# Two transformer blocks on one core: spreading the convolution's taps, two divisions and the weight splits over the attention loop by another table

## The chip, the cores and the metric

The kernel runs on one core of one Trainium2 chip. The metric is the device time of one execution in microseconds (us). Of the kernel before there are three timed runs, 1228.01, 1232.46 and 1233.43 us, with the median 1232.46 us. One further execution was profiled and took 1230.22 us. The engines are called TensorE (PE in the profile, PEld for its weight loads), VectorE (DVE), ScalarE (ACT), GpSimd (POOL) and SyncE (SP, which here only issues DMAs). The five engines run their own instruction queues in order and meet at semaphores only.

## The reference, cut to what matters

The program computes a first block (a gated pool and a chunked recurrence), and a second block on its output. The change lies in the second block's mixer, where an attention of 8 heads over 768 keys and a depthwise convolution of 31 taps over 512 channels are independent of one another until they meet in one projection:

```python
def dwconv(x, w, b):                       # k = 31 taps, 512 channels
    y = lax.conv_general_dilated(x, w[:, None, :], window_strides=(1,), padding=[(k // 2, k // 2)],
                                 dimension_numbers=('NWC', 'WIO', 'NWC'), feature_group_count=x.shape[-1])
    return y + b

def attend(q_nope, q_rope, k_nope, k_rope, v):
    s = (jnp.einsum('bqhd,bkhd->bhqk', q_nope, k_nope)
         + jnp.einsum('bqhr,bkr->bhqk', q_rope, k_rope)).astype(jnp.float32) * SOFTMAX_SCALE
    p = jax.nn.softmax(s, axis=-1).astype(v.dtype)
    return jnp.einsum('bhqk,bkhd->bqhd', p, v)

    attn_l = attend_blocked(q_nope_l, q_rope_l, ...)
    conv_l = conformer_conv(u_l, ...)      # silu(layer_norm(dwconv(a * sigmoid(g))))
    y_l = merge_groups(conv_l, attn_l, w_o[i], b_o[i])
```

## The kernel before, in words

Every engine has its own program, written out as a Python function that issues the engine's instructions in their final order; there is no scheduler. The attention is a loop over heads `h` 0 to 7 and six key tiles `t` 0 to 5 of 128 keys, and this pair (h, t), a step, is the unit in which work is placed on every engine.

TensorE computes in each step the scores of one key tile (three fp32r matmuls for the split operands, and a fourth that subtracts the row maximum through the diagonal tile DGR) and then multiplies the previous tile's exponentials (PR, which lie in PTA) with the values. In steps 1 to 4 it also computes two matmuls for the maxima of the next head (128 queries by 768 keys, tile PB). In step 2 it projects the queries of head h+2 (9 matmuls), in step 5 of an even head the keys of the next pair of heads (12 matmuls), and in steps (1, 3), (1, 4) and (2, 3) tiles of the values (12 short matmuls each). TensorE's program is not changed.

VectorE reduces the maxima (`maxima`, TENSOR_REDUCE of PB into PX), rotates the queries (`query`, TMPQ), computes the low halves of queries, keys and weights (HL, KL, WL; `split` is the weights' one and follows ScalarE's copy of the high half, WH), divides the finished pairs of heads (`pair`), and fills what is left with taps of the convolution (SCALAR_TENSOR_TENSOR on CV, one instruction per tap and group of 128 channels, 124 in all, 88 of them in this loop). How many taps follow each step is a table, `conv_step`; `conv_plan` deals the taps out in that order, alternating between two channel groups as long as there are two. Four places matter. The maxima of head h+1 for query tile j use one pair of PSUM banks for all j, so TensorE's maxima matmuls j+1 wait until VectorE has reduced j. The first score matmul group of head h+1 ends with DGR, which ScalarE makes from VectorE's fourth reduction of head h. The query projection in an odd head writes the bank from which VectorE reads `key_low(h + 2)`, and so waits for it. And `conv("end")` leaves nothing over: the last tap is at (7, 2).

ScalarE computes the exponential of each step (`power_of`, PTA), DGR (`maxima`), the high halves (KH, HH, WH), the copies of finished heads (`values_out`), and for each pair of heads the reciprocal of the denominators as Exp(-Ln(x)) (`divisors`), for which it loads one activation table and then the other back. `conv_square` squares a finished channel group two steps after its last tap (`CONV_END`), and GpSimd then adds the sums of groups 1 and 2 on VP and DG.

SyncE fetches the weight blocks; it waits for VectorE's splits (semaphore v_w), three buffers ahead.

Of the kernel before, what the change touches and what calls it, by code (L numbers as in the profile page):

```python
# [355 lines left out]
def build_in(nc, ctx, A, out, consts, masks):  # L356
# [152 lines left out]
    def raw_of(n):  # L509
        return RAW[n % NRAW]  # L510
# [44 lines left out]
    GLU_AT = {1: "82", 2: "84", 3: "86"}  # L555

    def conv_step(h, t):
        return 5 if h == 7 else (3, 2, 1, 1, 1, 3)[t] if h % 2 == 0 else (2, 1, 2, 1, 2, 3)[t]

    def conv_plan():  # L560

# [199 lines left out]
    def act_prog(e):  # L761
        a = Eng(e)

        def split(nb):

            if nb >= len(BLOCKS):
                return
            n, at, size = BLOCKS[nb]
            a.wait_ge(S_.raw[n % NRAW], n)
            if nb >= NW:  # L770
                a.wait_ge(S_.p_blk, nb - NW)
            a.copy(WH[nb % NW][:, 0:size], raw_of(n)[:, at:at + size]).then_inc(S_.a_w, nb)
# [367 lines left out]
        def key_high(h):  # L1140

            for part, (lo, hi) in enumerate(((NCTX, NKEY), (0, NCTX))):
                a.wait_ge(S_.p_blk, KEY_BLOCK[h // 2])
                if h > 2:
                    a.wait_ge(S_.p_sm, ("s", h - 3, 5))
                z = main.of(("k", h // 2, part))
                op = a.copy(KH[h % 3][0:64, lo:hi], z[64 * (h % 2):64 * (h % 2) + 64, 0:hi - lo])
            op.then_inc(S_.a_h, ("k", h))

        def query_high(h):  # L1150
            a.wait_ge(S_.v_ev, ("q", h))
            if h > 2:
                a.wait_ge(S_.p_sm, ("s", h - 3, 5))
            a.copy(QH[h % 3], TMPQ[:, :]).then_inc(S_.a_h, ("q", h))

        def value_tiles(g, q):
            if q < 2:
                a.wait_ge(S_.p_sm, ("v", g, q))
            else:
                a.wait_ge(S_.p_blk, VALUE_BLOCK[g])  # L1160
            a.wait_ge(S_.v_h, ("cq", 2))
            a.wait_ge(S_.v_h, ("kr", 2))
            z = main.of(("v", g, q))
            for i in range(2):
                op = a.copy(VGs[:, 2 * q + i, 2 * g:2 * g + 2, 0:3:2, :],
                            z[:, 256 * i:256 * i + 256].rearrange("p (a s n) -> p a s n", a=2, s=2))
            op.then_inc(S_.a_ev, ("v", g, q))

        def maxima(h, j):

            c = 4 * (h % 2) + j
            a.wait_ge(S_.v_ax, ("mx", h, j))
            if h > 1:
                a.wait_ge(S_.p_sm, ("s", h - 2, 5))
            a.act(DGR[h % 2][:, js(j)], IDN[:, :], ACTF.Identity, scale=NM[:, c:c + 1]).then_inc(S_.a_s, ("dgr", h, j))

        def power_of(h, t):
            s = 6 * h + t
            a.wait_ge(S_.p_sm, ("s", h, t))
            if s > 2:  # L1180
                a.wait_ge(S_.p_sm, ("o", (s - 3) // 6, (s - 3) % 6))
            a.act(PR[s % 3], main.of(("s", h, t)), ACTF.Exp, scale=SCALE).then_inc(S_.a_ev, ("s", h, t))

        def values_out(h):

            me, other = ((0, 64), (64, 128)) if h % 2 == 0 else ((64, 128), (0, 64))
            z = aux.of(("ov", h))
            a.wait_ge(S_.p_sm, ("o", h, 5))
            i = h // 2 % 2
            if h > 3:  # L1190
                a.wait_ge(S_.v_h, ("m", 4 + h // 2 - 2))
            a.copy(OTS[i][me[0]:me[1], :], z[me[0]:me[1], :])
            a.copy(SU[i][me[0]:me[1], :], z[other[0]:other[1], :]).then_inc(S_.a_ax, ("ov", h))

        def divisors(*pairs):

            for p in pairs:
                a.wait_ge(S_.a_ax, ("ov", 2 * p + 1))
                a.act(SU[p % 2], SU[p % 2], ACTF.Ln).then_inc(S_.a_s, ("sul", p))
            for p in pairs:  # L1200
                a.wait_ge(S_.a_s, ("sul", p))
                a.act(SU[p % 2], SU[p % 2], ACTF.Exp, scale=-1.0).then_inc(S_.a_s, ("su", p))

        def pair_high(p):
            a.wait_ge(S_.v_s, ("pair", p))
            a.copy(MH[:, 4 + p, :], OTS[p % 2]).then_inc(S_.a_h, ("m", 4 + p))

        def conv_square(j):
            a.wait_ge(S_.v_cv, ("cv", j))
            if j == 0:  # L1210
                a.wait_ge(S_.p_sm, "rqd")
            if j > 1:
                a.wait_ge(S_.g_cv, ("n2", min(j, 3) - 1))
            a.act(DG[:, :] if j else VP[:, 0, 0:512], CV[:, j, :], ACTF.Square).then_inc(S_.a_cv, ("sq", j))
# [18 lines left out]
        for h in range(8):  # L1233
            for t in range(6):
                power_of(h, t)
                if t == 0 and h % 2 and h < 6:
                    key_high(h + 2)
                    split(KEY_BLOCK[(h + 1) // 2] + NW)
                if t == 1 and h:
                    values_out(h - 1)  # L1240
                if 1 <= t <= 4 and h < 7:
                    maxima(h + 1, t - 1)
                if t == 4 and h in (3, 5):
                    pair_high((h - 3) // 2)
                if t == 3 and h < 6:
                    split(QUERY_BLOCK[h + 2] + NW)
                if t == 4 and h < 6:
                    query_high(h + 2)
                if (h, t) in ((1, 4), (1, 5), (2, 4)):
                    value_tiles(1, (h + t) - 5 if h == 1 else 2)  # L1250
                if (h, t) == (2, 4):
                    split(VALUE_BLOCK[1] + NW)
                if t == 5 and h in (2, 4):
                    divisors(h // 2 - 1)
                if t == 5 and h % 2 == 0 and h < 6:
                    key_high(h + 2)
                for j in range(4):
                    if CONV_END[j] != "end" and 6 * CONV_END[j][0] + CONV_END[j][1] + 2 == 6 * h + t < 44:
                        conv_square(j)
# [79 lines left out]
    def dve_prog(e):  # L1339
        v = Eng(e)  # L1340

        def split(nb):

            if nb >= len(BLOCKS):
                return
            n, at, size = BLOCKS[nb]
            v.wait_ge(S_.a_w, nb)
            i = nb % NW
            v.tt(WL[i][:, 0:size], raw_of(n)[:, at:at + size], WH[i][:, 0:size].bitcast(F32), SUB).then_inc(S_.v_w, nb)
# [450 lines left out]
        def query(h):  # L1800

            v.wait_ge(S_.p_blk, QUERY_BLOCK[h])
            if h:
                v.wait_ge(S_.v_h, ("q", h - 1))
            v.tt(TMPQ[:, :], main.of(("q", h)), CS[:, NCTX:NKEY], MUL).then_inc(S_.v_ev, ("q", h))
# [4 lines left out]
        def key_low(h):  # L1810
            v.wait_ge(S_.a_h, ("k", h))
            for part, (lo_, hi) in enumerate(((NCTX, NKEY), (0, NCTX))):
                z = main.of(("k", h // 2, part))[64 * (h % 2):64 * (h % 2) + 64, 0:hi - lo_]
                v.tt(KL[h % 3][0:64, lo_:hi], z, KH[h % 3][0:64, lo_:hi].bitcast(F32), SUB)\
                    .then_inc(S_.v_ev, *[("k", h // 2, part)] * (h % 2), *[("kl", h)] * part)

        def maxima(h, j):
            c = 4 * (h % 2) + j
            v.wait_ge(S_.p_sm, ("mx", h, j))
            if h > 1:  # L1820
                v.wait_ge(S_.a_s, ("dgr", h - 2, j))
            v.maxneg(NM[:, c:c + 1], PB[2 + (j % 2 if h == 0 else 0)][:, 0:NKEY]).then_inc(S_.v_ax, ("mx", h, j), ("mx2", h, j))

        def pair(p):

            v.wait_ge(S_.a_s, ("su", p))
            v.tt(OTS[p % 2], OTS[p % 2], SU[p % 2], MUL).then_inc(S_.v_s, ("pair", p))
# [18 lines left out]
        for h in range(8):  # L1846
            for t in range(6):
                if 1 <= t <= 4 and h < 7:
                    maxima(h + 1, t - 1)
                if t == 0 and h % 2 and h < 6:  # L1850
                    key_low(h + 1)
                    split(KEY_BLOCK[(h + 1) // 2] + NW)
                if t == 1 and h % 2 and h < 6:
                    key_low(h + 2)
                if t == 3 and h in (3, 5):
                    pair((h - 3) // 2)
                if t == 3 and h < 6:
                    query(h + 2)
                    split(QUERY_BLOCK[h + 2] + NW)
                if t == 5 and h < 6:  # L1860
                    query_low(h + 2)
                if t == 5 and h in (3, 5):
                    pair_low((h - 3) // 2)
                if t == 5 and h == 2:
                    split(VALUE_BLOCK[1] + NW)
                conv((h, t))
# [697 lines left out]
```

## Time and profile before

| | before |
|---|---|
| median of three runs | 1232.46 us |
| the profiled execution | 1230.22 us, span 1228.4 us |
| TensorE busy, weight loads busy | 1139.7 us (93%), 928.2 us (76%) |
| VectorE busy | 864.3 us (70%) |
| ScalarE busy | 550.5 us (45%) |
| GpSimd busy | 164.4 us (13%) |
| attention loop | about 660 to 797 us of the span |

Busy times are shares of one span and say nothing of a single stage. The attention loop takes 137 us, about 11% of the span; in the timeline of the trace a step can be told by its value matmul, the row PB<-PTA,VG, which starts after the scores of the step that follows.

### The profile page before, as it was taken

To read this page: it belongs to the slowest core of one execution; us is meant where nothing else is said; L and a number is where in the kernel's file an instruction comes from. 1 tells how busy PE (TensorE), PEld (TensorE's weight loads), DVE (VectorE), ACT (ScalarE), POOL (GpSimd) and SP (SyncE) were. 2 spreads that over 40 slices of the span, in tenths; PEclk is the share of its full clock that TensorE was granted. 3 is DMA by queue.
4 is the path that set the end of the run, shared out by engine and by line. 5 is a ranking of instruction groups with operands and counts; after the bars stand their busy time and mean duration, and the time that the engine had idled before them with its cause. 6 is when DMAs were issued, how large, how long until landed. Compare 5 with 4: busy or idle time off the path is not lost.

```text
span 1228.4 us, 14076 instructions
## 1 busy us (share of the span) xinstructions
PE 1139.7 (93%) x5488; PEld 928.2 (76%) x5488; DVE 864.3 (70%) x1352; ACT 550.5 (45%) x851; POOL 164.4 (13%) x179
## 2 busy tenths in 40 slices
PE   1869999999999989989999988998999999999996
PEld 1658888888888868879887755577888888888885
DVE  5868899988877774464888887967666656655236
ACT  3265455445433342776425565454643444432221
POOL 0034433344423210010010000000000000000001
PEclk9999999999999999999999999999999999999999
DMA  7723233233244566563211010112232222234211
GB/s 291 303 107 138 75 132 137 73 134 137 103 146 163 190 244 144 194 36 109 73 45 46 3 66 35 35 34 103 91 116 87 86 102 103 104 103 164 94 35 68
DMA packets 28306, 136.59 MB, mean 111 GB/s; under 512 B 7760, under 2 KB 8016, under 8 KB 14416
## 3 DMA queue, kind: packets, MB, share of 16 engines
q1 hardware_dynamic: 20448, 128.46, 29.8%
q10 hardware_dynamic: 7792, 7.24, 2.6%
q8 instruction: 43, 0.70, 0.2%
q14 instruction: 23, 0.19, 0.0%
HBM read 133.57 MB, written 2.12 MB: 110 GB/s over the span
## 4 chain that ended last, share of the span: by engine, by line
PE 66%; DVE 16%; ACT 10%; DMA 3%; issue 3%; POOL 1%; ACTq 0%; DVEq 0%; SPq 0%
PE PB L185 66%; DVE RAW L1365 3%; ACT WH L199 2%; ACT L200 2%; DMA RAW<-in_wstream 2%; DVE WL L206 2%; DVE CV L214 1%; DVE XL L214 1%; DVE SS L214 1%; DVE PX L237 1%; DMA XL<-in_xT 1%; DVE HB L231 1%; POOL UPA L206 1%; PE PB L193 1%; ACT HH L199 1%
## 5 line engine op out<-in xcount | busy, mean ns | idle before, releaser
L185 PE MATMUL PB<-HH,WH 128*128 128x512 f32 (+1 forms) x896 | 354.3, 395 | 18.8 <-DVE WL L206 8.3
L206 DVE TENSOR_TENSOR WL<-RAW,WH 128x1024 fp32r<-128x1024 f32 (+2 forms) x174 | 202.6, 1172 | 203.9 <-ACT WH L199 203.2
L185 PE MATMUL PB<-HH,WL 128*128 128x512 f32 (+1 forms) x896 | 343.6, 384 | 0.0
L185 PE MATMUL PB<-HL,WH 128*128 128x512 f32 (+1 forms) x896 | 343.4, 383 | 0.0
L199 ACT ACTIVATE WH<-RAW 128x1024 fp32r<-128x1024 f32 (+2 forms) x174 | 169.5, 981 | 297.5 <-PE PB L185 263.0
L185 PEld LDWEIGHTS PB<-HH,WH 128*128 128x128 f32 x896 | 171.6, 192 | 54.4 <-DVE WL L206 9.0
L185 PEld LDWEIGHTS PB<-HH,WL 128*128 128x128 f32 x896 | 171.2, 191 | 33.4
L185 PEld LDWEIGHTS PB<-HL,WH 128*128 128x128 f32 x896 | 171.8, 192 | 29.3 <-issue 0.5
L214 DVE SCALAR_TENSOR_TENSOR CV<-VP,PC,CV 128x512 f32<-128x512 f32 x120 | 89.1, 778 | 0.7
L206 POOL TENSOR_TENSOR PX<-PX,NPOW 128x2 f32<-128x2 f32 (+2 forms) x7 | 6.2, 893 | 474.7 <-DVE PX L206 428.4
L185 PE MATMUL PB<-WH,AH 128*128 128x512 f32 x176 | 68.5, 389 | 0.0
L185 PE MATMUL PB<-WL,AH 128*128 128x512 f32 x176 | 68.5, 389 | 0.0
L185 PE MATMUL PB<-WH,AL 128*128 128x512 f32 x176 | 68.5, 389 | 0.0
L206 POOL TENSOR_TENSOR PTA<-HB 128x256 f32<-128x256 f32 (+1 forms) x53 | 46.3, 898 | 124.4 <-DVE HB L231 112.3
L1365 DVE CUSTOM_DVE_ANT_0 RAW<-RAW,CR,PC 128x1024 f32<-128x1024 f32 x48 | 62.1, 1309 | 0.0
L185 PE MATMUL PB<-PTA,VG 128*128 128x512 f32 x96 | 51.5, 621 | 7.0 <-ACT PTA L200 7.0
L200 ACT ACT_TABLE_LOAD x43 | 55.2, 1283 | 6.1 <-DMA PC<-in_params 5.4
L185 PE MATMUL PB<-WH,HH 128*128 128x512 f32 x128 | 51.9, 406 | 2.2 <-DVE WL L206 1.4
L206 POOL TENSOR_TENSOR UPA<-HB 128x256 f32<-128x256 f32 (+1 forms) x51 | 45.0, 907 | 50.8 <-DVE HB L231 41.3
L200 ACT ACTIVATE PTA<-PTA 128x512 f32<-128x512 f32 x51 | 32.0, 627 | 42.4 <-POOL PTA L206 40.7
L185 PE MATMUL PB<-WL,HH 128*128 128x512 f32 x128 | 50.4, 394 | 0.0
L185 PE MATMUL PB<-WH,HL 128*128 128x512 f32 x128 | 50.3, 393 | 0.0
(270 smaller groups left out, 1855.1 us busy)
## 6 DMA issues: line engine op xcount, KB each, us to landing
RAW<-in_wstream SPq DMA_DIRECT2D x108, 1024.0 KB, 4.8
RAW<-in_wstream SPq DMA_DIRECT2D x5, 768.0 KB, 4.2
RAW<-in_wstream SPq DMA_DIRECT2D x5, 512.0 KB, 3.5
XL<-in_xT SPq DMA_DIRECT2D x2, 1024.0 KB, 8.1
HB<-in_x SPq DMA_DIRECT2D x2, 1024.0 KB, 6.3
out<-XL SPq DMA_DIRECT2D x8, 256.0 KB, 2.0
ROWS<-in_rows ACTq DMA_DIRECT2D x3, 512.0 KB, 7.9
XC<-in_ctx SPq DMA_DIRECT2D x1, 1024.0 KB, 7.0
```

Source lines behind the costliest of these rows:

```text
L185: return self.put(lambda e: e.matmul(o, l, r, start=start, stop=stop, skip_group_check=skip))
L193: return self.put(lambda e: e.transpose(o, i, idn))
L199: return self.put(lambda e: e.activation(o, i, f))
L200: return self.put(lambda e: e.activation(o, i, f, bias=bias, scale=scale))
L206: return self.put(lambda e: e.tensor_tensor(o, a, b, op))
L214: return self.put(lambda e: e.scalar_tensor_tensor(out=o, in0=a, scalar=s, in1=b, op0=o1, op1=o2))
L231: return self.put(lambda e: e.tensor_tensor_scan(o, a, b, 0.0, MUL, ADD))
L237: return self.put(lambda e: e.tensor_reduce(o, i, AX.X, ALU.max, negate=True))
L1365: v.put(lambda e: e.tensor_tensor_reduce(out=PROD if vec == "cc" else w, in0=w, in1=ROW[vec], scale=1.0, scalar=col(bias, j + i), op0=MUL, ...
```

## The change

In one table and two loops the change moves work; it adds and removes no instruction of the computation.

```diff
     def conv_step(h, t):
-        return 5 if h == 7 else (3, 2, 1, 1, 1, 3)[t] if h % 2 == 0 else (2, 1, 2, 1, 2, 3)[t]
+        return 5 if h == 7 else (2, 2, 5 if h < 6 else 2, 0, 1, 4)[t] if h % 2 == 0 else (1, 1, 5, 0, 1, 2)[t]
```

ScalarE's loop:

```diff
                 power_of(h, t)
+                if t == 2 and h in (2, 4):
+                    divisors(h // 2 - 1)
...
-                if t == 4 and h in (3, 5):
-                    pair_high((h - 3) // 2)
+                if t == 5 and h in (2, 4):
+                    pair_high(h // 2 - 1)
...
-                if t == 5 and h in (2, 4):
-                    divisors(h // 2 - 1)
```

VectorE's loop:

```diff
-                if t == 3 and h in (3, 5):
-                    pair((h - 3) // 2)
+                if t == 4 and h in (2, 4):
+                    pair(h // 2 - 1)
                 if t == 3 and h < 6:
                     query(h + 2)
+                if t == 4 and h < 6:
                     split(QUERY_BLOCK[h + 2] + NW)
                 if t == 5 and h < 6:
                     query_low(h + 2)
-                if t == 5 and h in (3, 5):
+                if t == 0 and h in (3, 5):
                     pair_low((h - 3) // 2)
```

The first place is VectorE's queue in head 3, from the second reduction for head 4 (step 2) to the first reduction for head 5 (in head 4, step 1). Before:

```order
L237 TENSOR_REDUCE PX<-PB 128x1
L214 SCALAR_TENSOR_TENSOR CV<-VP,PC,CV 128x512 x2
L237 TENSOR_REDUCE PX<-PB 128x1
L206 TENSOR_TENSOR OT<-OT,TMP 128x512
L206 TENSOR_TENSOR TMPQ<-PB,CS 128x512
L206 TENSOR_TENSOR WL<-RAW,WH 128x1024
L214 SCALAR_TENSOR_TENSOR CV<-VP,PC,CV 128x512
L237 TENSOR_REDUCE PX<-PB 128x1
```

In the changed kernel, the same stretch:

```order
L237 TENSOR_REDUCE PX<-PB 128x1
L211 TENSOR_SCALAR CV<-VP,PC 128x512
L214 SCALAR_TENSOR_TENSOR CV<-VP,PC,CV 128x512 x4
L237 TENSOR_REDUCE PX<-PB 128x1
L206 TENSOR_TENSOR TMPQ<-PB,CS 128x512
L237 TENSOR_REDUCE PX<-PB 128x1
L206 TENSOR_TENSOR WL<-RAW,WH 128x1024
L214 SCALAR_TENSOR_TENSOR CV<-VP,PC,CV 128x512
L206 TENSOR_TENSOR HL<-TMPQ,HH 128x512
L214 SCALAR_TENSOR_TENSOR CV<-VP,PC,CV 128x512 x4
L237 TENSOR_REDUCE PX<-PB 128x1
```

Five taps instead of two stand between the second and the third reduction; the fourth reduction has passed the division (OT), the split of a weight block (WL) and a tap; and four taps instead of six stand ahead of the first reduction for the next head (before, that stretch reads HL<-TMPQ, HL<-OT, six taps, TENSOR_REDUCE).

The second place is ScalarE's queue around the divisions of the first pair. Before, at the end of head 2 and the begin of head 3 (PTA<-PB is a step's exponential, TMP holds the denominators):

```order
L200 ACTIVATE PTA<-PB 128x512
L200 ACT_TABLE_LOAD
L200 ACTIVATE TMP<-TMP 128x512
L200 ACT_TABLE_LOAD
L200 ACTIVATE TMP<-TMP 128x512
L199 ACTIVATE KH<-PB 64x512
L199 ACTIVATE KH<-PB 64x256
L200 ACTIVATE PTA<-PB 128x512
```

In the changed kernel, at steps (2, 2) and (2, 3):

```order
L200 ACTIVATE PTA<-PB 128x512
L200 ACT_TABLE_LOAD
L200 ACTIVATE TMP<-TMP 128x512
L200 ACT_TABLE_LOAD
L200 ACTIVATE TMP<-TMP 128x512
L200 ACTIVATE DGR<-IDN,PX 128x128
L200 ACTIVATE PTA<-PB 128x512
L200 ACTIVATE DGR<-IDN,PX 128x128
```

The two table loads and two activations no longer stand between the last exponential of head 2 and the keys' high halves and first exponential of head 3; they stand between the exponentials of steps 2 and 3 of head 2. The same holds for head 4.

## Rows read from the trace of the kernel before

**Rows 1.** Windows: stretch and its length, busy (count) by engine, granted clock, DMA:

```profile
660.00:797.00 137.00, 124.98 (x467) 82.21 (x465) 112.58 (x155) 71.77 (x138) 5.83 (x4) 0.98 0.11 39
...
755.50:759.50 4.00, 3.98 (x9) 2.60 (x10) 2.69 (x5) 3.38 (x6) 0.00 (x0) 0.59 0.00 0
```

**Rows 2.** Waits of TensorE's matmuls, 659 to 797 us (total, times, longest):

```profile
PE PB L185 <- ACT PTA L200: 7.0, 4, 3.0
PE PB L185 <- DVE PX L237: 2.8, 4, 1.0
PE PB L185 <- ACT DGR L200: 2.7, 3, 0.9
```

**Rows 3.** Timeline of TensorE: start, us, instruction [idle before, releaser]:

```profile
693.07 1.02 PE L185 MATMUL PB<-PTA,VG 128*128 128x512 f32 x2
...
694.85 1.02 PE L185 MATMUL PB<-PTA,VG 128*128 128x512 f32 x2
...
696.99 1.02 PE L185 MATMUL PB<-PTA,VG 128*128 128x512 f32 x2
...
701.22 1.02 PE L185 MATMUL PB<-PTA,VG 128*128 128x512 f32 x2
...
704.77 1.02 PE L185 MATMUL PB<-PTA,VG 128*128 128x512 f32 x2
...
706.91 1.02 PE L185 MATMUL PB<-PTA,VG 128*128 128x512 f32 x2
...
710.82 1.02 PE L185 MATMUL PB<-PTA,VG 128*128 128x512 f32 x2
...
714.69 1.10 PE L185 MATMUL PB<-PTA,VG 128*128 128x512 f32 x2 [1.93 <-ACT PTA L200]
...
731.08 1.70 PE L185 MATMUL PB<-PTA,VG 128*128 128x512 f32 x2 [1.02 <-ACT PTA L200]
...
750.54 1.02 PE L185 MATMUL PB<-PTA,VG 128*128 128x512 f32 x2
...
755.52 2.05 PE L185 MATMUL PB<-PTA,VG 128*128 128x512 f32 x2 [3.04 <-ACT PTA L200]
...
773.11 1.12 PE L185 MATMUL PB<-PTA,VG 128*128 128x512 f32 x2 [1.03 <-ACT PTA L200]
...
786.30 1.02 PE L185 MATMUL PB<-PTA,VG 128*128 128x512 f32 x2
...
796.64 0.80 PE L185 MATMUL PB<-WH,HH 128*128 128x512 f32 x1
```

**Rows 4.** Timeline of VectorE:

```profile
691.93 4.06 DVE L214 SCALAR_TENSOR_TENSOR CV<-VP,PC,CV 128x512 f32<-128x512 f32 x6
...
718.66 1.03 DVE L206 TENSOR_TENSOR KL<-PB,KH 64x512 fp32r<-64x512 f32 x2
...
726.31 1.22 DVE L206 TENSOR_TENSOR WL<-RAW,WH 128x1024 fp32r<-128x1024 f32 x1 [0.22 <-ACT WH L199]
727.45 0.74 DVE L214 SCALAR_TENSOR_TENSOR CV<-VP,PC,CV 128x512 f32<-128x512 f32 x1
728.12 0.95 DVE L237 TENSOR_REDUCE PX<-PB 128x1 f32<-128x768 f32 x1
...
731.79 6.08 DVE L214 SCALAR_TENSOR_TENSOR CV<-VP,PC,CV 128x512 f32<-128x512 f32 x6
```

**Rows 5.** Timeline of ScalarE:

```profile
709.45 1.28 ACT L200 ACT_TABLE_LOAD   x1
...
713.96 0.58 ACT L200 ACTIVATE PTA<-PB 128x512 f32<-128x512 f32 x1
...
729.10 0.40 ACT L200 ACTIVATE DGR<-IDN,PX 128x128 fp32r<-128x128 f32 x1 [2.34 <-DVE PX L237]
```

**Rows 6.** Timeline of GpSimd:

```profile
731.62 1.38 POOL L206 TENSOR_TENSOR VP<-CV 128x512 f32<-128x512 f32 x1 [101.26 <-ACT DG L200]
732.96 1.72 POOL L206 TENSOR_TENSOR VP<-VP,DG 128x512 f32<-128x512 f32 x1
```

## The prediction

> **What bounds the kernel now.** I read the windows first. In the attention loop TensorE is busy for 125.0 of 137 us and VectorE for 112.6 [rows 1]; neither is full, and they must be holding one another up. The waits of TensorE's matmuls name three releasers: ScalarE's exponentials (PTA, 7.0 us in 4 waits), VectorE's reductions (PX, 2.8) and ScalarE's diagonals (DGR, 2.7), 12.5 us together [rows 2]. That is not all that is lost: after the longest wait, 3.04 us, the value matmul takes 2.05 us instead of 1.02 [rows 3], and in that stretch the granted clock is 0.59, that is, for most of it the lower of the two levels, 1.2 GHz [rows 1].
>
> The whole loss comes out of TensorE's timeline, by the starts of the value matmuls [rows 3]. The first four are a head at its own pace: a plain step takes 694.85 - 693.07 = 1.78 us, one with the matmuls of the next maxima 696.99 - 694.85 = 2.14, and one that also projects queries 701.22 - 696.99 = 4.23. A tile of values adds 704.77 - 701.22 - 2.14 = 1.41, and the keys add 710.82 - 706.91 - 1.78 = 2.13. So a head with nothing in its way takes 2 x 1.78 + 3 x 2.14 + 4.23 = 14.2 us if odd, 16.3 if even (keys), and head 6, which projects nothing, 2 x 1.78 + 4 x 2.14 = 12.1. Head 2 (16.3 + 1.41 = 17.7) took 710.82 - 693.07 = 17.75: no loss. Head 3 took 731.08 - 710.82 = 20.3, 6.0 too much. Head 4 took 19.5, 3.1 too much. Head 5 took 22.6, 8.3 too much. Head 6 took 13.2, 1.1 too much. Head 7, from 786.30 to the first matmul of the output projection at 796.64, has no waits. The loss is 18.5 us, all of it from head 3 on, and the change can gain no more than about that.
>
> **The change part by part.** It adds and removes no work on any engine, so a gain can only come from these 18.5 us.
>
> The divisions. Each of the two in the loop costs ScalarE two table loads of 1.28 us and two activations of about 0.63, 3.8 us in a row [rows 5]. Before, they stand ahead of the next head's first exponential, which starts at 713.96 and holds TensorE at 714.69 for 1.93 us; in head 5 the same costs 3.04 us and the low clock behind it [rows 3, 5]. They also hold up the keys' high halves, and behind these VectorE. At step 2 they have cover: the exponential of step 3 is only due 4.23 us after that of step 2. ScalarE does 0.6 us of exponential, 3.8 of divisions and one diagonal of 0.3, is done 4.7 us after it began, thus 0.5 late, and the result is needed one step (2.14 us) later. Cost nil; without that cover it would be 1.5 us twice. VectorE's `pair` at step 4 comes 5 us after the division is ready.
>
> The weight split. Before, split, tap and wait for ScalarE's copy stand between third and fourth reduction: the fourth starts at 728.12, its diagonal at 729.10, and TensorE waits for it 0.9 us in heads 3 and 5 (the third such wait of rows 2 is at the loop's begin), followed by 1.0 us for exponentials queued behind the diagonal (at 731.08 and 773.11) [rows 2 to 5]. Behind the change only the query's rotation (0.6) stands there, and the reduction starts as soon as its matmuls are done. The waits for the diagonal go. SyncE's next fetch waits for the split, which comes one step later; the loop uses 0.11 of the DMA engines' time [rows 1], and the blocks are used a head or more later, so I cost this at 0. If it did show, it would be a wait of at most one step, 2 us.
>
> The taps. What counts is VectorE's own work by head, now that it hardly waits for others. One tap takes 4.06 / 6 = 0.68 us. The rows of VectorE overlap their successors by 0.08 (726.31, 727.45, 728.12), so a reduction costs 0.87, a large split 1.14, a pair of key low halves 0.95 and a 128x512 subtraction or product about 0.61 [rows 4]; the smaller split in head 3 I put by its size at 0.5. Head 3: 10 taps 6.8, 4 reductions 3.5, keys 1.9, splits 1.6, query and two low halves 1.8 = 15.6. Head 4: 14 taps 9.5, 3.5, one split 1.1, query, pair and low half 1.8 = 15.9. Head 5 as head 3 with two large splits: 16.3. So in head 4 VectorE fits below TensorE's 16.3, and in heads 3 and 5 it needs more than the 14.2.
>
> Where it shows there: take head 5 with its first scores done at 0. In head 4 the fourth reduction can start at 11.7, and behind it stand 0.87, `pair` 0.6, the split 1.14, a tap 0.68, the query's low half 0.6 and four taps 2.7, so VectorE is done at 18.3, 2.0 after TensorE has begun head 5. It then does 0.95 of keys, 1.14 split, 0.61 `pair_low`, 0.68 tap: the first reduction starts at 5.4, where TensorE would have had it at 3.2. TensorE's second maxima matmuls are due at 4.8 and start when that reduction has ended, at 6.4; the query projection waits besides for the keys' first low half, until 7.0 instead of 5.1: 1.9 us lost. Then one tap, reduction at 7.9, five taps, third reduction at 12.2: the fourth maxima matmuls are due at 13.0 and start at 13.2, 0.15 lost. ScalarE's diagonal after that reduction, then its copy of the split's block (1.0), and only then the exponential of step 4: it ends 0.5 after TensorE wants it. Head 5 loses 1.9 + 0.15 + 0.55 = 2.6 instead of 8.3. The same walk for head 3, with the smaller split, gives 0.9 at the query projection and 0.55 at the exponential.
>
> But head 3 has one thing more. Channel group 1 now ends at (3, 0), so its square comes at (3, 2), and GpSimd's two additions fall into the five taps. Where GpSimd ran from 731.62 to 734.68, six taps took 6.08 us instead of 4.06 [rows 4, 6]. In the walk of head 3 the third reduction would start at 11.2 and is wanted by 11.05; with 2.0 us more it starts at 13.2, and TensorE's fourth maxima matmuls are 2.1 late. Head 3 loses 0.9 + 2.1 + 0.55 = 3.6. Bounds for what the additions cost VectorE: 0 (they find it in the reduction, which reads PSUM), and 3.1, their whole time. The Trainium skill, SBUF — State Buffer, section "SBUF: two separate sides", says that a GpSimd instruction and a VectorE one with two SBUF inputs lock each other out for their whole length. By that rule alone the price would be nearer 3.1 and the sum 1 us worse; the row shows 2.0, and 2.0 stands in the sum.
>
> Head 6 has group 2's additions at (6, 2) now, with two taps there and 0.4 slack to the third reduction: 1.0 lost, between 0 and 2.0, against 1.1 before. Head 4 loses nothing: its first reduction is due at 3.8 and VectorE, up to 2.1 late, reaches it after two taps at 3.5. The end: 10 taps are left behind the last reduction instead of 15, so VectorE is done well before TensorE; before, it finished just behind, but the projection's first block (5.5 us) covered it. No gain there. The chain behind the loop begins with ScalarE's copy of the last head and is unchanged.
>
> Sum of the losses after: 3.6 + 0 + 2.6 + 1.0 = 7.2, against 18.5: 11.3 us gained. As a check, VectorE's work in heads 3 to 5 is 15.6 + 2.0 + 15.9 + 16.3 = 49.8 us, and TensorE's heads in the forecast 17.8 + 16.3 + 16.8 = 50.9: VectorE is then full there. From the profiled execution that is 1230.2 - 11.3 = 1218.9; from the median, which lies 2.2 higher, 1221.2. I take 1220.0.
>
> **The rivals.** (A) All the waits go: GpSimd's additions and VectorE's lateness in the odd heads are absorbed in slack. 1230.2 - 18.5 = 1211.7. For it: TensorE sets the pace in heads 0 to 2 already. Against it: 16.3 us of VectorE work in a head of 14.2.
>
> (B) Half: five taps in one piece are too long. With 0.5 us of slack in an even head, none in an odd one, each us that VectorE is late at the third reduction comes straight onto TensorE, and ScalarE's exponential behind the block's copy doubles it. If taps in this place cost the row's own 0.74 instead of 0.68 (0.3 for five) and ScalarE is 0.5 later, heads 0 to 5 lose another 0.8 each: 1220 + 4.8 = 1225.
>
> (C) No change worth telling: the two divisions in heads 2 and 4 make exponentials late after all (1.5 twice), head 3 with the additions loses 5 instead of 3.6, and heads 0 to 2, where there is little to gain, lose 1.2 each: 3.0 + 1.4 + 3.6 = 8 us back, 1228.
>
> (D) Slower: TensorE's clock. After the stall at 755.52 the clock was low for most of 4 us, and the value matmul took twice its time; the one at 731.08 took 1.70 [rows 1, 3]. Now the stalls are shorter but lie in both odd heads, at the second maxima, the fourth and the exponential within 6 us. If TensorE fell to 1.2 GHz at each such place and stayed there through heads 3 to 6, a step would cost up to 1.8 more; from 7 such steps on the gain of 11.3 is gone, and with 10 it is 1218.9 + 18 = 1237. Against it: 1.93 us of wait at 714.69 left the next value matmul at 1.10 [rows 3]. The Trainium skill, TensorE: Matmul & The Clock Gate, Part 1, has just the two levels too and calls the lower one the state after idling.
>
> That the change doesn't do what it says I leave out: the order of the queues shows the moves.
>
> **How the numbers follow.** My forecast (1215 to 1223.5) has 0.62, A (1210 to 1215) 0.12, B (1223.5 to 1226.3) 0.12, C 0.08, D 0.06. Faster by over 0.5% means below 1226.3, about what a measurement of this kernel can tell: 0.62 + 0.12 + 0.12 = 0.86; same 0.08; slower 0.06. The range that leaves out D, most of C and the lower part of A is 1213 to 1227.
>
> **What would show it.** Right: no wait for DGR, and the exponentials' waits short, none over 1 us, in the first step of heads 3 and 5; heads 4 and 6 at 16.3 and about 13 us; heads 3 and 5 at 17 to 18; VectorE without idle over 0.5 us in heads 3 and 5; TensorE's waits naming PX at the second and fourth maxima matmuls; GpSimd's first additions within five taps of head 3; the loop ending about 785 instead of 797. Wrong: heads 3 and 5 at 20 us or more, waits of heads 0 to 2, or low clock in more than one stretch of heads 3 to 6.

## The result, and the profile after

The changed kernel took 1217.16 us in the median of four runs (1213.69 to 1218.24), the kernel before 1230.34 us in four (1228.01 to 1233.43): 13.2 us less, a ratio of 0.9875 with a 95% interval of 0.9852 to 0.9897. The ratio is taken from the record and is not the quotient of these two medians, which is 0.9893 and lies within the interval. Run again later, beside 13 executions of the kernel before (e11 below), the ratio was 0.9896 (0.9877 to 0.9914). The prediction was 1220.0 us, with a range of 1213 to 1227. The profiled execution of the changed kernel took 1213.69 us, the shortest of the four, span 1211.9.

Windows of the changed kernel (stretch and its length, busy us and count of PE, PEld, DVE, ACT, POOL, then granted clock, DMA share, GB/s), the first from the end of head 1 to the end of the loop, the second around the longest stall:

```profile
687.46:778.58 91.12, 87.13 (x327) 57.43 (x326) 80.45 (x112) 54.99 (x101) 6.16 (x4) 1.00 0.13 46
...
716.00:724.00 8.00, 5.99 (x21) 3.31 (x20) 7.89 (x10) 3.73 (x7) 1.68 (x2) 1.00 0.00 0
```

The clock is at the higher level of the two throughout. Before it fell in two stretches, to a mean of 0.59 from 755.5 us [rows 1] and, in head 4, to this one:

```profile
732.00:736.00 4.00, 4.00 (x10) 2.42 (x10) 4.00 (x4) 1.47 (x4) 2.67 (x2) 0.64 0.00 0
```

The waits of TensorE's matmuls in the changed kernel from 659 to 797 us, to be held against [rows 2]:

```profile
PE PB L185 <- DVE PX L237: 3.2, 3, 1.7
PE PB L185 <- ACT PTA L200: 0.6, 2, 0.3
PE PB L185 <- DVE HL L206: 0.5, 1, 0.5
```

The exponentials, 7.0 us before, are down to 0.6, and the diagonals are gone from this window (the one at the start of the loop, 0.86 us at 654.38, now lies ahead of it). The wait for HL comes at 788.58, behind the loop. TensorE's timeline, with the value matmul that ends each head and the first matmul of the output projection, answers to [rows 3]:

```profile
687.46 1.02 PE L185 MATMUL PB<-PTA,VG 128*128 128x512 f32 x2
...
705.21 1.02 PE L185 MATMUL PB<-PTA,VG 128*128 128x512 f32 x2
...
710.42 0.62 PE L185 MATMUL PB<-KH,HH 128*128 128x512 f32 x2 [0.26 <-DVE PX L237]
...
719.15 0.62 PE L185 MATMUL PB<-KH,HH 128*128 128x512 f32 x2 [1.71 <-DVE PX L237]
...
721.01 1.12 PE L185 MATMUL PB<-PTA,VG 128*128 128x512 f32 x2 [0.30 <-ACT PTA L200]
722.90 1.02 PE L185 MATMUL PB<-PTA,VG 128*128 128x512 f32 x2
...
739.32 1.02 PE L185 MATMUL PB<-PTA,VG 128*128 128x512 f32 x2
...
745.44 0.61 PE L185 MATMUL PB<-KH,HH 128*128 128x512 f32 x2 [1.18 <-DVE PX L237]
...
754.21 1.12 PE L185 MATMUL PB<-PTA,VG 128*128 128x512 f32 x2 [0.32 <-ACT PTA L200]
756.11 1.02 PE L185 MATMUL PB<-PTA,VG 128*128 128x512 f32 x2
...
768.24 1.02 PE L185 MATMUL PB<-PTA,VG 128*128 128x512 f32 x2
...
778.58 0.80 PE L185 MATMUL PB<-WH,HH 128*128 128x512 f32 x1
```

Differences of the starts that end heads (687.46, 705.21, 722.90, 739.32, 756.11, 768.24) are the heads. L, from the end of head 1 to the first matmul of the output projection, is what the experiments are measured by. Of the steps that the change touches, only those of heads 0 and 1 lie outside it. In two executions of the changed kernel L came out as 91.12 and 91.11 us, while whole times of one kernel spread over 2 to 9 us. Of the kernels whose loop runs in part at the low clock (before, e1, e3, e6 and e10) there is one profile each, so that their L repeats as well is not shown.

| us | head 2 | head 3 | head 4 | head 5 | head 6 | head 7 | L |
|---|---|---|---|---|---|---|---|
| before | 17.75 | 20.26 | 19.46 | 22.57 | 13.19 | 10.34 | 103.57 |
| forecast | 17.7 | 17.8 | 16.3 | 16.8 | 13.1 | 10.3 | 92.0 |
| changed kernel | 17.75 | 17.69 | 16.42 | 16.79 | 12.13 | 10.34 | 91.12 |

The loop gives 12.45 us in L and 0.4 in head 1 (17.47 before, 17.05 now). The two profiled executions differ by more (16.5), because the part ahead of the loop, which is the same code, was 5.1 us shorter in this one and the part behind it 1.6 longer; the second profile of the same kernel has the loop 4 us later (first value matmul at 659.74 instead of 655.79). That is scatter, not the change.

VectorE and GpSimd in head 3 of the changed kernel, against [rows 4, 6]:

```profile
712.12 0.96 DVE L237 TENSOR_REDUCE PX<-PB 128x1 f32<-128x768 f32 x1
713.00 0.54 DVE L211 TENSOR_SCALAR CV<-VP,PC 128x512 f32<-128x512 f32 x1
713.45 4.77 DVE L214 SCALAR_TENSOR_TENSOR CV<-VP,PC,CV 128x512 f32<-128x512 f32 x4
718.15 0.94 DVE L237 TENSOR_REDUCE PX<-PB 128x1 f32<-128x768 f32 x1
```

```profile
714.12 1.88 POOL L206 TENSOR_TENSOR VP<-CV 128x512 f32<-128x512 f32 x1 [88.88 <-ACT DG L200]
715.96 1.71 POOL L206 TENSOR_TENSOR VP<-VP,DG 128x512 f32<-128x512 f32 x1
```

Four taps take 4.77 us instead of the 2.73 they take elsewhere, 2.0 us more, under GpSimd's two additions, and TensorE's fourth maxima matmuls wait 1.71 us for the reduction behind them. One by one, two of the four taps take their usual 0.74 us, and these two take the rest:

```profile
714.78 1.77 DVE L214 SCALAR_TENSOR_TENSOR CV<-VP,PC,CV 128x512 f32<-128x512 f32 x1
...
716.47 1.75 DVE L214 SCALAR_TENSOR_TENSOR CV<-VP,PC,CV 128x512 f32<-128x512 f32 x1
```

### The profile page after: what moved, and what is told of

Same layout as the page of the kernel before. It is cut to its first block, busy times and chain, and to the rows that moved or that the text cites. A ratio compares the mean times of both kernels' runs of the same rounds, so it can differ in the third digit from the quotient of the medians.

```text
span 1211.9 us, 14076 instructions
## 1 busy us (share of the span) xinstructions
PE 1133.1 (94%) x5488; PEld 925.6 (76%) x5488; DVE 860.9 (71%) x1352; ACT 550.8 (45%) x851; POOL 165.3 (14%) x179
## 4 chain that ended last, share of the span: by engine, by line
PE 64%; DVE 18%; ACT 9%; DMA 4%; issue 3%; POOL 1%; ACTq 0%; DVEq 0%; SPq 0%
PE PB L185 63%; DVE RAW L1365 4%; ACT WH L199 3%; DMA RAW<-in_wstream 2%; ACT L200 2%; DVE WL L206 2%; DVE CV L214 2%; DVE XL L214 1%; DVE SS L214 1%; DMA vectors<-PX 1%; DVE HL L206 1%; DMA XL<-in_xT 1%; DVE HB L231 1%; PE PB L193 1%; POOL UPA L206 1%
## 5 line engine op out<-in xcount | busy, mean ns | idle before, releaser
L185 PE MATMUL PB<-HH,WH 128*128 128x512 f32 (+1 forms) x896 | 353.3, 394 | 18.5 <-DVE WL L206 8.0
L214 DVE SCALAR_TENSOR_TENSOR PTA<-PB,PC,PTA 128x511 f32<-128x511 f32 x66 | 49.2, 747 | 1.2
```

Of the source, the lines that this page charges most:

```text
L185: return self.put(lambda e: e.matmul(o, l, r, start=start, stop=stop, skip_group_check=skip))
L214: return self.put(lambda e: e.scalar_tensor_tensor(out=o, in0=a, scalar=s, in1=b, op0=o1, op1=o2))
```

## The experiments

Each ratio is to executions of the kernel before that ran beside it; their medians are 1230.99 us for e1 to e4, 1231.31 for e5 to e8 and 1233.02 for e9 to e12. The L of each experiment comes from one profile.

**One part undone (e1 to e3).** e1 leaves the divisions where they were, e2 the weight split, e3 the table:

```diff
 # e1, against the changed kernel (and pair, pair_high, pair_low likewise)
-                if t == 2 and h in (2, 4):
+                if t == 5 and h in (2, 4):
                     divisors(h // 2 - 1)
 # e2
                     query(h + 2)
-                if t == 4 and h < 6:
                     split(QUERY_BLOCK[h + 2] + NW)
 # e3
-        return 5 if h == 7 else (2, 2, 5 if h < 6 else 2, 0, 1, 4)[t] if h % 2 == 0 else (1, 1, 5, 0, 1, 2)[t]
+        return 5 if h == 7 else (3, 2, 1, 1, 1, 3)[t] if h % 2 == 0 else (2, 1, 2, 1, 2, 3)[t]
```

> The new table and the later weight splits, with the divisions (and pair, pair_high, pair_low) where they were before. Measure: L, from the value matmul that ends head 1 to the first matmul of the output projection (before 103.6 us, changed kernel 91.1 us in their profiles). Theory (the losses are local, each tied to one part; the divisions held TensorE by 1.9 and 3.0 us, then by late keys and the low clock): L comes back to 97 to 99 us, with waits for exponentials at the first step of heads 3 and 5. Rival (the table does the work, since VectorE's load is what bounds heads 3 and 5): L stays below 93 us.

Measured: L 95.61 us (head 3 20.26, head 5 18.12), median 1222.44 us, ratio to before 0.9943 (0.9925 to 0.996). Between the two expectations: the divisions cost 4.5 us here, not 6 to 8. TensorE's waits in e1:

```profile
720.05 1.86 PE L185 MATMUL PB<-PTA,VG 128*128 128x512 f32 x2 [1.92 <-ACT PTA L200]
...
755.91 1.10 PE L185 MATMUL PB<-PTA,VG 128*128 128x512 f32 x2 [0.74 <-ACT PTA L200]
```

In head 3 the wait is the one of before, 1.9 us, with a value matmul of 1.86 us behind it (the clock's mean was 0.72 from 720 to 726 us). In head 5 it is 0.74 instead of 3.04. The division's first table load before (first line) and in e1 (second), and the value matmul that ends head 4 in e1, show why:

```profile
750.28 1.28 ACT L200 ACT_TABLE_LOAD   x1
...
750.66 1.28 ACT L200 ACT_TABLE_LOAD   x1
...
753.23 1.02 PE L185 MATMUL PB<-PTA,VG 128*128 128x512 f32 x2
```

Before, the division starts 0.26 us ahead of that matmul (750.54 [rows 3]); in e1 it starts 2.57 us ahead and runs beside TensorE's projection of the keys. Lead and wait add up to 3.3 us both times. The rival is refuted, the theory right in place and too high in price.

> The new table and the early divisions, with the query blocks' weight split at step 3 ahead of the fourth reduction, as before. Theory: the fourth reduction starts 1.8 us later in heads 3 and 5 (it waits for ScalarE's copy of the block and the split), the diagonal and the exponentials behind it cost 1.6 us in each of the two heads, nothing in the even heads where the key projection covers it: L about 94.5 us. Rival (the split only changed places with idle time): L 91 us.

Measured: L 93.69 us (head 3 18.62, head 5 18.18, the even heads 16.55 and 12.24), median 1220.65, ratio 0.9923 (0.9896 to 0.995). 0.9 and 1.4 us in the two odd heads, little elsewhere: place as expected, sum 2.6 instead of 3.4.

> Early divisions and late weight splits with the old table of taps. Theory (VectorE's queue is full in heads 3 to 5 either way, and the table only moves where it is late; GpSimd's additions then fall at the begin of head 4): L 90 to 92 us, the table is worth 0 to 1 us in this company. Rival (the table was the larger part): L 94 us or more.

Measured: L 98.3 us, median 1221.95, ratio 0.9927 (0.9906 to 0.9949). The theory fell: by L, the table is worth 7.2 us in this company. Head 3 was even faster than with the new table (15.56 us), head 4 took 22.55, and heads 5 and 6 took 1.5 and 1.6 us more than in the changed kernel. VectorE, GpSimd and TensorE of e3 at the start of head 4, then its clock there:

```profile
724.59 6.13 DVE L214 SCALAR_TENSOR_TENSOR CV<-VP,PC,CV 128x512 f32<-128x512 f32 x6
730.64 0.94 DVE L237 TENSOR_REDUCE PX<-PB 128x1 f32<-128x768 f32 x1
```

```profile
723.86 1.96 POOL L206 TENSOR_TENSOR VP<-CV 128x512 f32<-128x512 f32 x1 [96.36 <-ACT DG L200]
725.78 1.74 POOL L206 TENSOR_TENSOR VP<-VP,DG 128x512 f32<-128x512 f32 x1
```

```profile
731.64 1.01 PE L185 MATMUL PB<-KH,HH 128*128 128x512 f32 x2 [3.22 <-DVE PX L237]
732.45 0.63 PE L185 MATMUL PB<-CH,WH 128*128 128x512 f32 x1
```

```profile
731.00:735.00 4.00, 3.36 (x8) 2.69 (x9) 3.44 (x5) 3.33 (x5) 0.00 (x0) 0.50 0.00 0
```

The old table ends channel group 1 at (3, 3), so the additions meet six taps in a row with no reduction between them; TensorE, no longer late for other reasons, waits 3.22 us for the reduction behind, and then runs at 1.2 GHz for the whole of the next 4 us. What I had left out of the expectation was that a TensorE that comes earlier waits longer for the same VectorE: at this place it waits 1.04 us before, 2.14 with the divisions alone (e6) and 3.22 here.

**Without the additions (e4, e5).** The changed kernel and e3, with GpSimd's additions for group 1 cut short:

```diff
-                g.tt(S1_, CV[:, 0, :], CV[:, 1, :], ADD).then_inc(S_.g_cv, ("n1", j))
+                g.tt(S1_[:, 0:4], CV[:, 0, 0:4], CV[:, 1, 0:4], ADD).then_inc(S_.g_cv, ("n1", j))
...
-            g.tt(S2_, S2_, DG[:, :], ADD).then_inc(S_.g_cv, ("n2", j))
+            w = 4 if j == 1 else 512
+            g.tt(S2_[:, 0:w], S2_[:, 0:w], DG[:, 0:w], ADD).then_inc(S_.g_cv, ("n2", j))
```

> The changed kernel, with GpSimd's two additions for channel group 1 cut to 4 of their 512 columns (the sums of squares of the other columns are left out). Theory (the additions slow VectorE's taps in head 3 by 1.5 us and TensorE waits for it): head 3 takes 15.7 to 16.2 us instead of 17.7, L about 89.3 us. Rival (head 3 is slow by VectorE's load alone): L 91 us.

Measured: L 89.07 us, head 3 15.65, median 1214.07, ratio 0.987 (0.9843 to 0.9897). The place is as the theory had it, and the additions cost head 3 2.0 us, where it said 1.5.

> Early divisions, late splits, the old table of taps, and GpSimd's additions for group 1 cut to 4 of 512 columns (the sums of squares of the other columns are left out). The old table in this company lost 6.1 us in head 4, where the additions met six taps in a row. Theory (additions plus six taps make the long wait, and the wait the low clock): head 4 falls from 22.6 to 17 to 18 us, with the clock at 1 throughout, and L (from the end of head 1 to the output projection) from 98.3 to 92 to 93.5 us, so most of the table's worth is in where the additions fall. Rival (six taps in a row are enough by themselves): head 4 stays above 20 us.

Measured: L 92.12 us, head 4 17.87 (one execution, 1216.72 us), as the theory had it, and this wait in the place of the 3.22, with the clock's mean at 1.00 from 691 to 783 us:

```profile
730.52 0.62 PE L185 MATMUL PB<-KH,HH 128*128 128x512 f32 x2 [1.13 <-DVE PX L237]
```

So of the 7.2 us that separate old and new table with the additions (98.3 and 91.1), 3.05 are there without them (92.12 and 89.07), 1.5 of it in head 4 and 1.7 in head 6, where the old table has six taps ahead of the first reduction (e5 waits 1.35 us there). The other 4.1 are what the additions and the low clock behind the longer wait cost in one place more than in the other. This rests on one profile each.

**One part alone (e6, e9, e10).** The same edits, each made alone to the kernel before.

> Only the early divisions (with pair, pair_high, pair_low), table and splits as before. The gains may not add up: the theory has the old table's six taps and the additions still at the begin of head 4, and VectorE decides there. Theory: heads 3 and 4 together 38 to 39 us (before 39.7, with the late splits as well 38.1), head 5 18 to 19 us, L 98 to 99.5 us. Rival (parts add up: the divisions were worth 4.5 us on top of the other two): L 99 us with head 3 at 18 or below and head 4 unchanged at 19.5.

Measured: L 97.6 us (heads 3 to 5: 17.42, 18.95, 20.3), median 1225.01, ratio 0.9951 (0.9931 to 0.997). 6.0 us, somewhat more than the theory allowed; heads 3 and 4 together 36.4, not 38 to 39, and head 5 slower than expected. The rival fails too: it wanted 4.5 us and head 4 unchanged.

> Only the new table of taps, divisions and splits as before. If the parts added up, the table would be worth what it was worth on top of the other two: 7.2 us, L 96.4 us (L from the end of head 1 to the output projection; before 103.6). Theory: it adds up only in part, since the divisions at the begin of heads 3 and 5 leave their waits (1.9 and 3.0 us, and in head 5 the low clock), while the additions now fall in head 3: head 3 20 to 21.5 us, head 4 16.4 to 17, head 5 19.5 to 21, L 97.5 to 99.5 us. Rival (five taps ahead of the third reduction, with the split ahead of the fourth, make it no better than before): L 102 us or more.

Measured: L 99.6 us (heads 3 to 5: 21.47, 16.61, 21.18), median 1225.51, ratio 0.9938 (0.9919 to 0.9956). 4.0 us, close above the theory's upper end. Head 4 is healed, heads 3 and 5 keep the divisions' waits, and head 3, where the additions now fall too, takes longer than before (21.47 for 20.26); in head 5, TensorE and its value matmul:

```profile
753.17 1.10 PE L185 MATMUL PB<-PTA,VG 128*128 128x512 f32 x2 [2.33 <-ACT PTA L200]
```

> Only the later weight splits, table and divisions as before. Theory: the waits for the diagonal (0.9 us in heads 3 and 5) and for the exponentials queued behind it (1.0 us each) go, the divisions and the additions with their low clock stay: L 99.5 to 101.5 us. Rival (parts add up: 2.6 us, what the splits were worth on top of the other two): L 101 us; the two cannot be told apart by L alone, but by which waits are left: theory no wait for DGR in the loop beyond the one at its start.

Measured: L 101.76 us, median 1231.01, ratio 0.9981 (0.9966 to 0.9996): 1.8 us in the loop, 0.3 above the theory's range. No wait for the diagonal is left beyond the one at the loop's start (0.9 us), but the time came back as another wait, in head 4, ahead of matmuls at the low clock (mean 0.57 from 737 to 741 us):

```profile
737.16 0.92 PE L185 MATMUL PB<-KH,HH 128*128 128x512 f32 x2 [3.36 <-DVE PX L237]
```

The eight combinations, L in us (D divisions, S splits, T table):

| none | S | T | D | S+T | D+T | D+S | D+S+T |
|---|---|---|---|---|---|---|---|
| 103.57 | 101.76 | 99.60 | 97.60 | 95.61 | 93.69 | 98.30 | 91.12 |

Alone the parts are worth 6.0 (D), 4.0 (T) and 1.8 (S) in L, 11.8 in sum, where the whole change gives 12.45; as the last part added, 4.5, 7.2 and 2.6. And the late splits on top of the divisions alone lose 0.7 in L (97.60 to 98.30): with the old table heads 3 and 5 get 1.9 and 2.0 us shorter, but head 4, with its wait and the low clock, 3.6 and head 6 0.9 longer.

The whole times do not confirm all of this. Below the median of the kernel before that ran beside it lie D by 6.3 us, T by 7.5, S by 2.0, D+S by 9.0 and the changed kernel by 12.9 (e11). The intervals are wide, but T's (5.4 to 10.0 us) and D+S's (6.3 to 11.6) leave out what their loops show, 4.4 and 5.3 with head 1. By these times the table would be worth 7.5 alone and 3.9 on top, and the late splits on top of the divisions would gain. Which is right for the table stays open: the figures from L rest on the single profiles of the kernel before and of e3, whose loops run in part at the low clock, and the whole times take in the scatter of everything outside the loop. What both show for the divisions, 6.0 alone and 4.5 on top (6.3 and 4.3), and for the splits (1.8 and 2.6; 2.0 and 2.5), agrees.

**A better place for the additions, and a lighter load in the odd heads (e7, e8).** e7 puts the squares of groups 1 and 2 off; e8 has another table besides:

```diff
+    SQUARE_AT = {0: (1, 1), 1: (6, 5), 2: (7, 2)}
...
-                    if CONV_END[j] != "end" and 6 * CONV_END[j][0] + CONV_END[j][1] + 2 == 6 * h + t < 44:
+                    if SQUARE_AT.get(j) == (h, t):
                         conv_square(j)
...
-            if CONV_END[j] == "end" or 6 * CONV_END[j][0] + CONV_END[j][1] + 2 >= 44:
+            if j not in SQUARE_AT:
                 conv_square(j)
 # e8 besides
-        return 5 if h == 7 else (2, 2, 5 if h < 6 else 2, 0, 1, 4)[t] if h % 2 == 0 else (1, 1, 5, 0, 1, 2)[t]
+        return ((2, 2, 5, 0, 1, 4), (1, 1, 5, 2, 1, 2), (4, 2, 5, 2, 1, 3), (1, 1, 4, 0, 1, 2),
+                (2, 2, 5, 0, 1, 2), (0, 1, 4, 0, 1, 2), (2, 2, 2, 0, 1, 4), (5,) * 6)[h][t]
```

> The changed kernel with the squares of channel groups 1 and 2, and with them GpSimd's additions, put off to steps (6, 5) and (7, 2), where VectorE has time left. Nothing is left out. Theory: head 3 falls to 15.7 us as with the cut additions, head 6 stays at 12.1, the end of the loop does not move since VectorE's last tap stays ahead of the output projection's first block: L 89.1 us, about 2 us faster than the changed kernel. Rival (the additions cost the same wherever they stand): L 91 us.

Measured: L 89.07 us, head 3 15.64, head 6 12.13, median 1214.23 (1213.01 to 1218.45), ratio 0.9865 (0.9834 to 0.9896). The additions do cost VectorE time again, ten taps 11.51 us instead of 7.83 in the changed kernel, but now where nobody waits for it. The 2.05 us against the changed kernel are seen in L; the ratio's interval takes in the changed kernel's 0.9875. VectorE's taps and the 8.24 us for which it is idle behind them:

```profile
765.80 11.51 DVE L214 SCALAR_TENSOR_TENSOR CV<-VP,PC,CV 128x512 f32<-128x512 f32 x10
785.55 0.69 DVE L206 TENSOR_TENSOR OT<-OT,TMP 128x512 f32<-128x512 f32 x1 [8.24 <-ACT TMP L200]
```

> As e7_late_squares, with another table: six taps taken from the ends of heads 2 and 4 and from heads 3 and 5, and given to heads 1 and 2, where VectorE idles at steps 3 and 0. Theory (in heads 3 and 5 TensorE now waits for VectorE's load alone): head 3 14.3 to 14.6, head 5 14.3 to 14.8, the others as they are, L 85.5 us, time near 1211.5 us. Rival (a lag of VectorE elsewhere, for instance the first reduction of head 2 or the third behind two more taps, takes it back): L 88 us or more.

Measured: L 87.12 us (head 3 14.91, head 5 15.44), median 1216.08 (1210.5 to 1219.1), ratio 0.9869 (0.9828 to 0.991). Between theory and rival: 2.0 us shorter than e7, not 3.6. In head 5 VectorE now waits for ScalarE's copy of the block that it splits:

```profile
744.45 1.23 DVE L206 TENSOR_TENSOR WL<-RAW,WH 128x1024 fp32r<-128x1024 f32 x1 [1.31 <-ACT WH L199]
```

The whole time did not show the 2 us; it scattered by 8.6 us over four runs. Hence the last two, side by side on one chip:

> The changed kernel once more, beside e12 on the same chip: L 91.1 us, ratio to the kernel before 0.987 to 0.990.

Measured: L 91.11 us, median 1220.16 us (1217.73 to 1222.0), ratio 0.9896 (0.9877 to 0.9914).

> The kernel of e8 once more, to place its time beside the changed kernel's: its loop was 4.0 us shorter. Theory (nothing outside the loop moves): 3 to 4.5 us faster than e11 in the median. Rival (given back behind the loop): within 1 us of e11.

Measured: L 87.11 us, median 1215.28 us (1212.16 to 1216.23), ratio 0.9847 (0.9827 to 0.9866). 4.9 us below e11 with no run in common, and intervals that don't meet: this version beats the kernel before and the changed one. The loop gives 4.0 of it; a spread of some us lies over the rest. That is a little above the theory's 3 to 4.5, and the rival is refuted.

## Why the prediction was right

The direction, the place and the size were right: 11.3 us forecast, 13.2 measured in the median, 12.45 in L. The whole time is the coarser test of the two, since the changed kernel's own median was 1217.16 us once and 1220.16 the other time; what supports the mechanism are the heads. Of the 1.2 us that L gave beyond the forecast, 1.0 is head 6. By its own steps:

- The loss before, 18.5 us from head 3 on, was the right frame. The change gave back 12.45 of it, and nothing outside the loop is shown to have moved.
- The divisions at step 2 cost nothing: no matmul waits for the exponential behind them in the changed kernel (the two waits of 0.30 and 0.32 us come at step 4, behind the weight block's copy). Moving them there was worth 6.0 us (e6) and 4.5 (changed kernel against e1). In the sum I named no price for each part, and these two figures show that the part has none of its own.
- The weight split: waits for the diagonal gone, as said; the DMA side at 0, with no wait for it named in any profile.
- The odd heads. Head 5 was put at 16.8 and took 16.79: TensorE waits 1.18 us and then 0.32 in the places named, the second maxima matmuls and the exponential of step 4. By the starts of the value matmuls step 2 lost 1.8 us and step 4 0.6, where 1.9 and 0.7 were forecast. Head 3 was put at 17.8 and took 17.69, with 2.0 us of GpSimd's additions as the largest term; e4 takes the additions away and gets 15.65.
- The Trainium skill, SBUF — State Buffer, section "SBUF: two separate sides", says that the loser waits for the other's whole instruction. The trace agrees once it is read tap by tap: the two long taps are 1.03 and 1.01 us above the usual 0.74, and the additions, 1.88 and 1.71 us by their rows, start while a tap is running that still takes 0.74 and 0.59 us, which leaves 1.14 and 1.12. So I had the right price, 2.0, but was wrong that the rule would make it nearer 3.1: the 3.1 us of the rows hold waits of GpSimd's own. That reductions from PSUM are left alone is in line with the page's condition of two SBUF inputs.
- Head 6 was mis-sized: 1.0 us of loss, none measured. The additions for group 2 ran from 763.61 to 766.21 us and met the end of a tap, two reductions of 0.95 and 0.96 us, their usual length, and idle time. That was the lower bound of that step; I had taken the middle.
- Head 1 I had put at no gain, and it gave 0.4: 17.47 to 17.05 us.
- Rival D, the low clock, did not come in the changed kernel, but it was a real mechanism: it came in e3 and e10 after waits of 3.2 and 3.4 us and in e6 after 2.31, at the second maxima matmuls as I had named, though in e3 and e10 in head 4 and not in an odd head. It lasted a few us each time, not through heads 3 to 6. Rival A (all the waits go) wanted heads 3 and 5 at 14.2. Rival B (five taps too long) and C (late exponentials) are refuted by heads 1, 2 and 4 (17.05, 17.75, 16.42).

What I had right for a reason that was incomplete is the table. The sum treated it as a shift of VectorE's lateness, and my expectation for e3 said in so many words that it was worth 0 to 1 us. By L it is worth 7.2 on top of the other parts, by the whole times nearer 4. In the traces it moves six taps in a row away from the first reduction (3.05 us without group 1's additions), and GpSimd's additions away from those six taps.

What stays open: the table's worth alone and on top of the rest, on which L and the whole times differ; the 1.9 us in heads 3 and 5 of e8 above the loop's own pace (VectorE's wait for ScalarE's copy is seen; moving that copy was not tried), and why head 3 of e1 ran at a low clock after a wait of 1.9 us while 2.33 us in e9 left it up.

## What to carry to other kernels

In a loop where two in-order engines hold each other up, add up the load of each by iteration, and put filler work where the other engine has its long pieces (here five taps beside the query projection), never in a row ahead of an instruction that the other waits for. Parts of such a change have no price of their own: an engine that comes earlier to the next place where it depends on the other waits longer there (1.04, 2.14 and 3.22 us at one place), so the divisions were worth 6.0 us alone and 4.5 on top of the others. Work on GpSimd that slows VectorE belongs where VectorE is ahead: putting it off by three heads was worth 2 us of the loop for a few lines of code. And a metric taken from one profile should be held against the whole times before a price is read from it.

## What the runs showed of the hardware

- Two GpSimd additions of 128x512 with SBUF operands (2.8 to 3.8 us together by their rows) lengthened VectorE's taps beside them by 2.0 to 2.1 us (4.77 for 2.73, 6.13 for 4.06, 4.87 for 2.73 in e1); 1.84 us per pair in e7 (11.51 for 7.83 with two pairs). Two taps carry it each time, about 1 us each. Reductions from PSUM beside the additions kept their 0.95 us.
- TensorE's granted clock fell to 1.2 GHz after waits of 3.0 to 3.4 us in every case seen (before, e3, e10). After shorter ones it went either way: down after 1.92 us in e1, after 2.31 us in e6 (mean 0.66 from 753 to 758 us) and, in the kernel before, after waits of 0.92 and 1.02 us close together (mean 0.64 from 732 to 736 us); up after 1.93 us and after another 0.92 and 1.03 us (at 771.59 and 773.11) in the kernel before, 1.71 in the changed one, 2.14 in e6 and 2.33 in e9. With the lower level in play one value matmul took 1.70 to 2.05 us instead of 1.02.
- A chain of taps on one channel group takes 0.78 us a tap (10 in 7.83 us), two groups by turns 0.68 (5 in 3.40).
